# Gates of 256 dense tokens added into device memory by indirect DMAs, and POOL's share of the weight halves cut at the 36th up block

## What is computed

```python
s1, i1 = lax.top_k(sc[:, :, 0], PEER_TOPK)          # 512 tokens, 8 heads, 16 of 128 keys
s2, i2 = lax.top_k(sc[:, :, 1], PEER_TOPK)
best, pos = lax.top_k(all_pairs(s1, s2), PEER_TOPK)  # 16 of the pairs
idx = e1 * PEER_NKEYS + e2                           # 16384 experts
gate = jax.nn.softmax(best, axis=-1)
act = jax.nn.gelu(jnp.einsum('phkd,pd->phk', u_tab[idx], t)) * gate
out = jnp.einsum('phk,phkd->pd', act, v_tab[idx])    # then added to x, and a last RMS norm
```

## Time and profile before

| | |
|---|---|
| median of 3 runs | 3638.95 us (3638.54 to 3649.3) |
| profiled execution | 3639.07 us |
| its span, first to last instruction | 3637.2 us |
| mean granted TensorE clock | 0.993 of full speed |
| TensorE busy | 3538.1 us (97%) |
| VectorE busy | 2284.6 us (63%) |
| ScalarE busy | 1472.4 us (40%) |
| POOL busy | 884.6 us (24%) |

### The profile page before, as it was taken

How to read it: one execution, slowest core, us unless ns; L and a number is a source line. 1 busy time by engine, 2 the same in 40 slices (tenths; PEclk the granted TensorE clock), 3 DMA queues, 4 the chain that set the end, 5 groups by cost and what they waited for, 6 DMA issues and landing times.

```text
span 3637.2 us, 56094 instructions
## 1 busy us (share of the span) xinstructions
PE 3538.1 (97%) x22572; PEld 3247.0 (89%) x22572; DVE 2284.6 (63%) x3965; ACT 1472.4 (40%) x2191; POOL 884.6 (24%) x795
## 2 busy tenths in 40 slices
PE   8999999999899999999998999999999999999998
PEld 8988999999797678788677877899999999999998
DVE  7445465554844545555687444479988885777775
ACT  7254453222625435222466444243333433333333
POOL 4010022111401012211213201035646662111110
PEclk9999999999999999999999999999999999999999
DMA  4212232222221123222222122348869999999894
GB/s 155 70 42 65 76 116 93 93 92 94 70 65 54 63 82 133 95 97 93 75 81 70 60 93 81 95 140 272 281 214 258 298 289 338 314 310 313 307 312 139
DMA packets 293617, 544.70 MB, mean 150 GB/s; under 512 B 138288, under 2 KB 187568, under 8 KB 292976
## 3 DMA queue, kind: packets, MB, share of 16 engines
q1 hardware_dynamic: 185248, 394.34, 32.6%
q0 software_dynamic: 27648, 100.68, 8.4%
q10 hardware_dynamic: 80464, 46.10, 4.3%
HBM read 483.67 MB, written 56.62 MB: 149 GB/s over the span
## 4 chain that ended last, share of the span: by engine, by line
PE 86%; DVE 8%; ACT 3%; issue 1%; POOL 1%; DMA 0%; ACTq 0%; DVEq 0%; POOLq 0%
PE PSM L317 19%; PE PSM L318 18%; PE PSM L319 18%; PE PSM L211 5%; PE PSM L3160 5%; PE PSM L3162 5%; PE PSM L3161 5%; PE PSM L3136 3%; DVE PARTS L284 2%; ACT PARTS L275 1%; PE PSM L1061 1%; DVE MH L1741 1%; PE PSM L825 1%; PE PSM L1097 1%; DVE QK L1375 1%
## 5 line engine op out<-in xcount | busy, mean ns | idle before, releaser
L284 DVE TENSOR_TENSOR PARTS<-RAW,PARTS 128x1024 fp32r<-128x1024 f32 (+1 forms) x612 | 743.8, 1220 | 476.4 <-ACT PARTS L275 476.2
L275 ACT ACTIVATE PARTS<-RAW 128x1024 fp32r<-128x1024 f32 x612 | 645.4, 1057 | 932.1 <-PE PSM L319 488.6
L317 PE MATMUL PSM<-UX,PARTS 128*128 128x264 f32 (+3 forms) x2912 | 987.1, 339 | 27.4 <-DVE UX L2297 4.9
L318 PE MATMUL PSM<-UX,PARTS 128*128 128x264 f32 (+3 forms) x2912 | 970.2, 333 | 0.0
L319 PE MATMUL PSM<-UX,PARTS 128*128 128x264 f32 (+3 forms) x2912 | 969.5, 333 | 0.0
L317 PEld LDWEIGHTS PSM<-UX,PARTS 128*128 128x128 f32 x2912 | 548.8, 188 | 78.4 <-issue 9.2
L318 PEld LDWEIGHTS PSM<-UX,PARTS 128*128 128x128 f32 x2912 | 549.0, 189 | 29.9 <-issue 1.7
L319 PEld LDWEIGHTS PSM<-UX,PARTS 128*128 128x128 f32 x2912 | 547.9, 188 | 29.7
L3160 PE MATMUL PSM<-AC,PARTS 128*128 128x416 f32 x1024 | 358.3, 350 | 2.3 <-DVE AC L3457 2.3
L3162 PE MATMUL PSM<-AC,PARTS 128*128 128x416 f32 x1024 | 357.6, 349 | 0.0
L3161 PE MATMUL PSM<-AC,PARTS 128*128 128x416 f32 x1024 | 357.5, 349 | 0.0
(11 more groups left out here) (516 smaller groups left out, 5815.9 us busy)
## 6 DMA issues: line engine op xcount, KB each, us to landing
RAW<-w_ff_dram SPq DMA_DIRECT2D x128, 512.0 KB, 3.2
RAW<-peer_u_dram SPq DMA_DIRECT2D x128, 512.0 KB, 4.8
RAW<-peer_v_dram SPq DMA_DIRECT2D x128, 512.0 KB, 5.1
RAW<-w_in_dram SPq DMA_DIRECT2D x116, 512.0 KB, 3.2
acts_dram<-MQ ACTq DMA_DIRECT2D x128, 208.0 KB, 4.2
MQ<-acts_dram SPq DMA_DIRECT2D x128, 208.0 KB, 3.8
MQ<-gates_dram SPq DMA_DIRECT2D x128, 208.0 KB, 4.7
RAW<-w_mix_o_dram SPq DMA_DIRECT2D x32, 512.0 KB, 3.3
```

The costliest lines, as they stand in the source:

```text
L275: e.activation(p[:, 0:1024], self.raw.of(i), ACT.Copy).then_inc(S.sem, S.tick("w", i))
L284: e.tensor_tensor(p[:, 1024:1024 + n], r[:, 0:n], p[:, 0:n].bitcast(F), SUB).then_inc(V.sem, V.tick("w", i))
L317: e.matmul(dst, wh[k], xh_[k][:, lo:hi], start=(k == 0), stop=False, skip_group_check=True)
L318: e.matmul(dst, wh[k], xl_[k][:, lo:hi], start=False, stop=False, skip_group_check=True)
```

## The change

Gates of tokens 0 to 255 (groups 0 and 1) are no longer made by one-hot products. In the second layer's feed-forward, ScalarE's queue stores zeros into that part of `gates_dram` (8 DMAs of 2 MB). When group 0 or 1 has been chosen, VectorE works out for each of its tokens and choices the place in `gates_dram` (`placed`, in blocks 34 and 52). POOL then issues 128 indirect DMAs for each group (`scatter`), each of which adds one number for each of 128 tokens to its place. Every sixteenth, except the first of a group, waits for all earlier ones of its group to have landed, since two heads may add to the same place. The 256 scatters are spread over blocks 36 to 121: 99 in blocks 36 to 68, 41 in blocks 69 to 89, 116 in blocks 90 to 121.

The fills drop from seven to three (tokens 384 to 415 and 256 to 383), in blocks 70 to 89; the turns of groups 0 and 1 go. POOL's share of the halves ends at block 35. Of the 96 up gathers and dots of the few tokens, the last 26 move into the down pass (`late`), ahead of the 96 sums there, in the same eight buffers; ScalarE's gelu for them moves to block 29 of that pass. `back(0)` waits for all 256 scatters.

```diff
-                self.pooled = {first["pu"] + i for i in range(5, 68)}
+                self.pooled = {first["pu"] + i for i in range(5, 36)}
...
+                if l == 1 and g < 8:
+                    if g == 0:
+                        e.wait_ge(G.sem, G.at("zeros"))
+                    src = zeros.unsqueeze(1).to_broadcast([128, 16, SCATTERED])
+                    e.dma_start(Gd[16 * g:16 * g + 16, :, 0:SCATTERED].rearrange("n p t -> p n t"), src).then_inc(zero_out, 16)
...
-        HERE = 46
-        FILLS = [(3, 384, 4)] + [(g // 2, 64 * g, 8) for g in range(6)]
-        FILL_AT = [70] + [74 + 8 * g for g in range(6)]
+        HERE, THERE = 46, 70
+        FILLS = [(3, 384, 4)] + [(g // 2, 64 * g, 8) for g in range(4, 6)]
+        FILL_AT = [70, 74, 82]
...
-            return [n for c, n in enumerate(ORDER) if i == 18 * c + 18]
+            return [n for c, n in enumerate(ORDER) if i == 18 * c + 18 and n >= 2]
+
+        def placed_at(i):
+            return [n for c, n in enumerate(ORDER) if i == 18 * c + 16 and n < 2]
+
+        def scatters_by(i):
+            for i0, i1, q0, q1 in ((36, 69, 0, 99), (69, 90, 99, 140), (90, 122, 140, 256)):
+                if i0 <= i < i1:
+                    return q0 + (q1 - q0) * (i + 1 - i0) // (i1 - i0)
+            return 0 if i < 36 else 256
...
-            return 21 + 45 * s_ // (HERE - 1) if s_ < HERE else 77 + 49 * (s_ - HERE) // (FEW - 1 - HERE)
+            return 21 + 45 * s_ // (HERE - 1) if s_ < HERE else 77 + 49 * (s_ - HERE) // (THERE - 1 - HERE)
...
+        def late(r):
+
+            return gv_[r % 8], gv_in[r % 8], r // 8 + 1
...
+        LATE = FEW - THERE
+        WHOLE = 6 + 114 * LATE // (FEW + LATE - 1)
+
+        def late_at(i):
+            return [r for r in range(FEW + LATE) if i == 6 + 114 * r // (FEW + LATE - 1)]
...
-                    e.wait_ge(g_out[0], 16 * 48)
-                if j % 8 == 0 and j < 64:
-                    e.wait_ge(g_last[j // 8], 16)
-                elif j == 64:
-                    e.wait_ge(g_out[1], 16 * 56)
+                    e.wait_ge(g_out[0], 16 * 16)
+                    e.wait_ge(g_out[1], 16 * 32)
+                    for placed in placed_out:
+                        e.wait_ge(placed, 16 * 128)
...
+                if i == WHOLE - 1:
+                    e.wait_ge(V.sem, V.at("dot", FEW - 1))
+                    for a, _, _ in few:
+                        e.activation(a, a, ACT.Gelu_apprx_tanh).then_inc(S.sem, S.tick("few"))
...
+            def placed(n):
+                e1, e2, gv = chosen_[n]
+                if n == 0:
+                    e.scalar_tensor_tensor(out=spot, in0=con["ident"], scalar=1.0, in1=iota, op0=MUL, op1=MUL,
+                                           accum_out=column[:, 0:1]).then_inc(V.sem, V.tick())
+                    e.wait_ge(V.sem, V.n)
+                    e.tensor_scalar(column[:, 1:2], column[:, 0:1], 128.0, None, ADD).then_inc(V.sem, V.tick())
+                e.tensor_copy(share_[n], gv).then_inc(V.sem, V.tick())
+                e.scalar_tensor_tensor(out=spot, in0=e2, scalar=128.0, in1=e1, op0=MUL, op1=ADD).then_inc(V.sem, V.tick())
+                e.wait_ge(V.sem, V.n)
+                e.scalar_tensor_tensor(out=spot, in0=spot, scalar=float(TD), in1=column[:, n:n + 1].to_broadcast([128, 128]),
+                                       op0=MUL, op1=ADD).then_inc(V.sem, V.tick())
+                e.wait_ge(V.sem, V.n)
+                e.tensor_copy(place_[n], spot).then_inc(V.sem, V.tick("placed", n))
...
+            def scatter(n, s_):
+                if s_ == 0:
+                    e.wait_ge(V.sem, V.at("placed", n))
+                    e.wait_ge(zero_out, 16 * 8)
+                elif s_ % 16 == 0:
+                    e.wait_ge(placed_out[n], 16 * s_)
+                e.indirect_dma_start(Gflat, bass.IndirectOffsetOnAxis(ap=place_[n][:, s_:s_ + 1], axis=0),
+                                     share_[n][:, s_:s_ + 1], None, compute_op=ADD).then_inc(placed_out[n], 16)
```

More of the change, by code:

```diff
@@ L152, in program @@
         g_out = [sem(f"g_out{i}") for i in range(2)]
-        g_last = [sem(f"g_last{i}") for i in range(8)]
+        zero_out = sem("zero_out")
+        placed_out = [sem(f"placed_out{i}") for i in range(2)]
         few_in = sem("few_in")
@@ L1675, in ff_pool @@
             n = TT - 16 * l
+            if l == 1:
+                e.memset(zeros, 0.0).then_inc(G.sem, G.tick("zeros"))
             for i in range(32):
@@ L1756, in program @@
         c2 = {n: sb(oC2 + o, w) for n, (o, w) in C2_OFF.items()}
+        SCATTERED = 256
+        zeros = sb(oT + 5120, SCATTERED)
         four = lambda o: [sb(o + i * 512, 512) for i in range(4)]
@@ L2943, in program @@
         chosen_ = [[CH[:, 384 * n + 128 * i:384 * n + 128 * i + 128] for i in range(3)] for n in range(4)]
-        sm = qb(place(16), 16)
+        sm = qb(place(32), 32)
         TD, FEW, HALVES = 416, 96, 64
@@ L2988, in program @@
         ORDER = [3, 0, 1, 2]
-        HERE = 46
-        FILLS = [(3, 384, 4)] + [(g // 2, 64 * g, 8) for g in range(6)]
-        FILL_AT = [70] + [74 + 8 * g for g in range(6)]
+        HERE, THERE = 46, 70
+        FILLS = [(3, 384, 4)] + [(g // 2, 64 * g, 8) for g in range(4, 6)]
+        FILL_AT = [70, 74, 82]
+        Gflat = Gd.rearrange("n p t -> (n p t)").unsqueeze(1)
+        place_ = [qb(oE1 + 128 * n, 128).bitcast(U32) for n in range(2)]
+        share_ = [qb(oGt + 128 * n, 128) for n in range(2)]
+        spot, column = qb(oE2, 128), sm[:, 16:18]
         def pieces_by(i):
@@ L3002, in turn_at, with scatters_at @@
         def turn_at(i):
-            return [n for c, n in enumerate(ORDER) if i == 18 * c + 18]
+            return [n for c, n in enumerate(ORDER) if i == 18 * c + 18 and n >= 2]
[6 more added lines that the diff above has]
+            return 0 if i < 36 else 256
+        def scatters_at(i):
+            return [(q // 128, q % 128) for q in range(scatters_by(i - 1), scatters_by(i))]
         def dots_at(i):
-            return [s_ for s_ in range(FEW) if i == dot_at(s_)]
+            return [s_ for s_ in range(THERE) if i == dot_at(s_)]
         def dot_at(s_):
-            return 21 + 45 * s_ // (HERE - 1) if s_ < HERE else 77 + 49 * (s_ - HERE) // (FEW - 1 - HERE)
+            return 21 + 45 * s_ // (HERE - 1) if s_ < HERE else 77 + 49 * (s_ - HERE) // (THERE - 1 - HERE)
         def rows(s_):
-            return (gu[s_ % 5], gu_in[s_ % 5], s_ // 5 + 1) if s_ < HERE else (
-                gu2[s_ % 3], gu_in[5 + s_ % 3], (s_ - HERE) // 3 + 1)
+            if s_ < HERE:
+                return gu[s_ % 5], gu_in[s_ % 5], s_ // 5 + 1
+            if s_ < THERE:
+                return gu2[s_ % 3], gu_in[5 + s_ % 3], (s_ - HERE) // 3 + 1
+            return late(s_ - THERE)
+        def late(r):
+            return gv_[r % 8], gv_in[r % 8], r // 8 + 1
         def gathers_at(i):
-            return [s_ for s_ in range(FEW) if i == (
+            return [s_ for s_ in range(THERE) if i == (
                 (18 if s_ < 5 else dot_at(s_ - 5) + 1) if s_ < HERE else (75 if s_ < HERE + 3 else dot_at(s_ - 3) + 1))]
-        def sums_at(i):
-            return [s_ for s_ in range(FEW) if i == 6 + 114 * s_ // 95]
+        LATE = FEW - THERE
+        WHOLE = 6 + 114 * LATE // (FEW + LATE - 1)
+        def late_at(i):
+            return [r for r in range(FEW + LATE) if i == 6 + 114 * r // (FEW + LATE - 1)]
         def group(s_):
@@ L3037, in out_sp @@
         def out_sp(i):
-            return [(f, c) for f in range(7) for c in range(8) if i == last_at(f) + 5 + 3 * c // 4]
+            return [(f, c) for f in range(3) for c in range(8) if i == last_at(f) + 5 + 3 * c // 4]
         def out_act(i):
-            return [(f, c) for f in range(7) for c in range(8, 16) if i == last_at(f) + 1 + 3 * (c - 8) // 4]
+            return [(f, c) for f in range(3) for c in range(8, 16) if i == last_at(f) + 1 + 3 * (c - 8) // 4]
         def half_of(f):
@@ L3070, in peer_sp @@
                     e.wait_ge(S.sem, S.at("gates", f, FILLS[f][2] - 1))
-                    e.dma_start(*gates_out(f, c)).then_inc(g_last[c] if f == 6 else g_out[half_of(f)], 16)
+                    e.dma_start(*gates_out(f, c)).then_inc(g_out[half_of(f)], 16)
                 if i >= NB:
@@ L3263, in peer_act @@
             store(NB - 1)
-            e.wait_ge(V.sem, V.at("dot", FEW - 1))
-            for a, _, _ in few:
-                e.activation(a, a, ACT.Gelu_apprx_tanh).then_inc(S.sem, S.tick("few"))
             for i in range(NB):
@@ L3417, in sum_ @@
                 w, c = group(s_)
-                x, a, y = gv_[s_ % 8], few[w][0][:, c:c + 1], few_y[w]
-                e.wait_ge(gv_in[s_ % 8], 16 * (s_ // 8 + 1))
+                x, landed, turn_ = late(LATE + s_)
+                a, y = few[w][0][:, c:c + 1], few_y[w]
+                e.wait_ge(landed, 16 * turn_)
                 if s_ == 0:
-                    e.wait_ge(g_out[1], 16 * 56)
-                    for done in g_last:
```

(31 more changed lines are left out.)

## The result

The changed kernel takes 3846.69 us (median of 4 runs, 3843.78 to 3850.57). The kernel before takes 3641.86 us in the same comparison. The ratio is 1.0553, with a 95% interval of 1.054 to 1.0566. That is 253 us above the forecast of 3594 us, and far outside its range. It ended on the side of the third rival.

What follows compares the result with a forecast made beforehand. TensorE, on 86% of the chain of waits, was taken as the bound. 3639.07 - 57.1 (gates) - 0.7 (turns) + 12.3 (VectorE's extra work) = 3594 us, with POOL and DMA charged nothing; range 3580 to 3643 us.

Steps and rivals of the forecast that it cites:

- the third rival: POOL's queue, block 36 to first gate load: accumulating scatter is dear, kernel slower; at 1.6 us each 3707 us; chance 0.15.
- The step that failed: POOL, blocks 36 to 121: each of 256 scatters priced like a gather, 1.03 us, bounds 0.95 and 1.2.
- the balance: POOL from block 36 to the first gate load: 297 us left for scatters, or 1.16 us for each of 256.
- TensorE's gain: Expert up pass: 32 of 52 gated blocks become plain, 57.1 us saved, and two turns go, 0.7 us.
- VectorE's cost: Blocks 36 to 67: whole halves and preparing places and shares give back 12.3 us, bounds 8 and 17.
- the sum of 16.8 us: VectorE, blocks 36 to 67: 18.3 us of added work where 1.5 us is idle leaves 16.8 us over.
- the lead of two blocks: VectorE makes halves two blocks ahead of TensorE; this swallows between nothing and 9 us, taken as 4.5 us.
- The waits: POOL's queue: 14 waits for earlier scatters to land, each between 1.1 and 5.3 us, taken as 3.2 us.
- What was charged at nothing: Added DMA packets, gathers and dots moved into the down pass, and zero stores were all taken as hidden.
- The DMA share: Blocks 36 to 68: scatter packets raise the queues' share from 0.82 to about 0.87 to 1.1; charged nothing.
- The down pass: 26 gathers and dots move in, 35 us of VectorE, DMA share about 0.97; hidden, 35 us if cover were gone.
- The zeros: Second feed-forward, ScalarE's queue: eight 2 MB stores, DMA share rises 0.12; charged nothing, bounded at 5 us in all.

## Why the prediction was wrong

**The step that failed** is "I take 1.03 us, bounds 0.95 and 1.2" for a scatter, read off the gather because both are one indirect DMA over 128 partitions. The term was 256 x 1.03 us; it measured 256 x (1.72 + 0.27) us. Two parts were missing. The adding costs 0.6 us an instruction, shown by leaving out the adding alone. The 0.30 us between indirect DMAs that follow one another do not stand in the gather's duration, and in the trace before only 12 of 96 gathers show them (2.8 us in all), since most had waited for another engine in that place. A third, smaller one is the excess over 1.55 us, 0.17 us on average. It was largest where VectorE was busiest: a mean of 1.93 us from 2540 to 2600, where VectorE is busy for 54 of 60 us, and of 1.63 us from 3060 to 3240, where it is busy for 35 of 180. That VectorE causes it was not tested. For this I had bounds from one kind of row only; the sentence "no row has an accumulating transfer" was the warning, and 0.15 was too small a chance for it, since the balance left room for 1.16 us only.

**The rival had the right mechanism, and its size was too small.** With 1.99 us it gives 3594 + (1.99 - 1.16) x 256 = 3806 us; 3847 were measured. Of the other 40 us about 16 are POOL's other work, which took longer than I charged (one-hots 76 us against 67, gathers about 59 against 52.5), 10 the 0.30-us gaps ahead of the gathers, and 10 the longer start of the down pass. Against that the waits for landing took 34 us where the rival counted 45. Some 15 us remain that I have not told apart.

**TensorE's gain was right.** Predicted 57.1 + 0.7 us; without scatters and with POOL's halves the up pass is 57.8 us shorter. That the last digit agrees is luck: the kernel's time fell by 52 us.

**VectorE's cost was nearly right.** Predicted 12.3 us, bounds 8 to 17; measured 16 us alone and 15 us in the change without scatters. Against the sum of 16.8 us, the lead of two blocks, which I let swallow 4.5 us, swallowed about nothing.

**The waits were right in size.** Predicted 3.2 us each; measured 34.3 us in 13, or 2.6. A scatter landed 2.9 to 7.9 us after its issue, 3.4 in the median. The Trainium skill ("DMA: Bandwidth & Descriptors", the section on the anatomy of one DMA) puts the fixed part of a DMA from POOL at about 2.0 us; a wait of about 1 us, the estimate by that figure, is further from the measurement than the 3.2 us from the rows. The same section of the Trainium skill counts the making of descriptors as small and variable. Here POOL's instruction took 1.55 us for an accumulating scatter, and no run shows how much of that is the making of descriptors.

**What was charged at nothing held.** The DMA share was 0.62 to 0.68 in the three stretches of the loss, so the packets were no bound, and the scatters of 64 partitions show the same. The down pass was 3.5 us longer in the run without scatters and with POOL's halves (581.1 against 577.6 us), and 0.6 us in the change. The zeros show no cost that stands out: the kernel with VectorE's halves alone, which has none, began the expert layer at 2371 us, the change at 2373.

## What to carry to other kernels

An engine with 24% busy time may have no room in the one stretch where the new work must go. Add up its queue there, and work out the price at which it fills: if the operation has no row of its own, as here the adding, take the nearest row as a floor and not as a middle, and give a price twice as high a fair chance. Work that leaves the engine on the chain is worth only what the queue that takes it over can carry, and in an in-order queue the first victim is whatever stands behind it, here a gather that had nothing to do with the gates.

## What was not expected of the hardware

At the least, an accumulating indirect DMA of 128 single numbers kept POOL for 1.54 us, the same one without adding for 0.95 us, and one of half the partitions for 1.40 us. By the counts of POOL's queue an accumulating scatter makes (64,512 - 27,648) / 256 = 144 packets, as many as a gather (27,648 / 192), and a writing one (35,840 - 27,648) / 256 = 32. The queue of the page, of the change and then of the writing scatter:

```profile
q0 software_dynamic: 64512, 100.82, 10.6%
```

```profile
q0 software_dynamic: 35840, 100.82, 8.3%
```

Indirect DMAs issued one behind the other stand 0.30 us apart on POOL in all three kinds that ran here: adding scatters (70.3 us in 239 gaps), writing ones (68.6 in 233) and gathers (10.0 in 33).
